# Weight halves of the FFN steps moved between the gate's operations on VectorE and ScalarE

## The reference

```python
def adaln_in(x, g, m, i):                       # first block
    return rmsnorm(x, g) * (1 + m[:, i, 1][:, None]) + m[:, i, 0][:, None]

def swiglu(h, w1, w3, w2):
    return (jax.nn.silu(h @ w1) * (h @ w3)) @ w2

m = (cond @ w_mod[l] + b_mod[l]).reshape(bsz, 3, 3, D_MODEL)
x = x + 0.5 * m[:, 0, 2][:, None] * swiglu(adaln_in(...), ffn_w1, ffn_w3, ffn_w2)   # first block
h = h + 0.5 * swiglu_2(rmsnorm_2(h, g[0]), ffn_w1, ffn_w3, ffn_w2)                  # second block
```

## Time and profile before

| | |
|---|---|
| median of 3 runs | 1780.08 us |
| the profiled execution | 1783.61 us, span 1781.8 us |
| TensorE (PE) busy | 1501.1 us, 84% |
| VectorE (DVE) busy | 1397.3 us, 78% |
| ScalarE (ACT) busy | 986.8 us, 55% |
| DMA | 420.30 MB, 236 GB/s in the mean |
| low halves (L1957) on VectorE | 418 of the pairs and 205 of block 2, about 1220 ns each |
| high halves (L1444) on ScalarE | 418 and 209, about 1046 ns each |

### The profile page before, as it was taken

How to read it: one execution, slowest core, us unless ns; L and a number is a source line. 1 busy time by engine, 2 the same in 40 slices (tenths; PEclk the granted TensorE clock), 3 DMA queues, 4 the chain that set the end, 5 groups by cost and what they waited for, 6 DMA issues and landing times.

```text
span 1781.8 us, 27728 instructions
## 1 busy us (share of the span) xinstructions
PE 1501.1 (84%) x11160; PEld 1416.2 (79%) x11160; DVE 1397.3 (78%) x2275; ACT 986.8 (55%) x1643; POOL 9.8 (1%) x24
## 2 busy tenths in 40 slices
PE   5988778788878888886998997997998899788997
PEld 4988667677868786866998997887998799767996
DVE  7598866789988998867888777786777777786776
ACT  4444535554555445536666556555555655675554
POOL 0000000000000000000000000000000000000000
PEclk8699878898988998998999998998999899899999
DMA  8599863579967994425896775336677577425763
GB/s 332 207 365 376 313 207 124 204 262 337 325 239 283 377 375 157 162 99 211 303 334 218 246 248 198 143 113 231 233 243 245 190 249 247 157 82 211 242 244 107
DMA packets 84972, 420.30 MB, mean 236 GB/s; under 512 B 9363, under 2 KB 9795, under 8 KB 58094
## 3 DMA queue, kind: packets, MB, share of 16 engines
q1 hardware_dynamic: 82910, 410.59, 63.6%
q0 software_dynamic: 1936, 7.95, 1.3%
HBM read 417.37 MB, written 1.13 MB: 235 GB/s over the span
## 4 chain that ended last, share of the span: by engine, by line
DVE 55%; ACT 16%; PE 16%; issue 6%; DMA 6%; SPq 0%; DVEq 0%
DVE low_p L1957 19%; DVE low_d L1957 11%; DVE modw L1790 7%; ACT hi_p L1444 6%; ACT a_hi L1467 4%; PE pw L624 4%; DVE gu L2085 3%; PE pw L625 3%; DVE gu L2077 3%; PE acc L624 3%; PE acc L625 3%; DMA land_p<-stream 2%; ACT gu L1462 2%; DMA land_d<-stream 2%; DMA biasT<-wmod 2%
## 5 line engine op out<-in xcount | busy, mean ns | idle before, releaser
L624 PE MATMUL pw<-h_hi,hi_p 128*128 128x256 f32 x2928 | 760.3, 297 | 129.7 <-DVE low_p L1957 113.2
L625 PE MATMUL pw<-h_lo,low_p 128*128 128x256 f32 x2928 | 739.8, 290 | 0.0
L624 PEld LDWEIGHTS pw<-h_hi,hi_p 128*128 128x128 f32 x2928 | 584.6, 200 | 166.2 <-DVE low_p L1957 116.2
L625 PEld LDWEIGHTS pw<-h_lo,low_p 128*128 128x128 f32 x2928 | 585.0, 200 | 0.4 <-issue 0.2
L1957 DVE SCALAR_TENSOR_TENSOR low_p<-hi_p,land_p 128x1024 fp32r<-128x1024 f32 x418 | 494.0, 1220 | 107.5 <-ACT hi_p L1444 107.4
L1444 ACT ACTIVATE hi_p<-land_p 128x1024 fp32r<-128x1024 f32 x418 | 418.1, 1045 | 90.0 <-DMA land_p<-stream 89.9
L624 PE MATMUL acc<-a_hi,hi_d 128*128 128x256 f32 x1376 | 357.0, 294 | 54.4 <-DVE low_d L1957 54.4
L625 PE MATMUL acc<-a_lo,low_d 128*128 128x256 f32 x1376 | 354.0, 292 | 0.0
L624 PEld LDWEIGHTS acc<-a_hi,hi_d 128*128 128x128 f32 x1376 | 278.1, 202 | 57.4 <-issue 57.4
L625 PEld LDWEIGHTS acc<-a_lo,low_d 128*128 128x128 f32 x1376 | 278.2, 202 | 0.0
L1957 DVE SCALAR_TENSOR_TENSOR low_d<-hi_d,land_d 128x1024 fp32r<-128x1024 f32 x205 | 249.5, 1218 | 9.2 <-ACT hi_d L1444 9.1
(11 more groups left out here) (354 smaller groups left out, 1723.6 us busy)
## 6 DMA issues: line engine op xcount, KB each, us to landing
land_p<-stream SPq DMA_DIRECT2D x207, 1024.0 KB, 5.1
land_d<-stream SPq DMA_DIRECT2D x209, 512.0 KB, 5.7
modw<-wmod SPq DMA_DIRECT2D x124, 512.0 KB, 5.7
biasT<-wmod SPq DMA_DIRECT2D x20, 512.0 KB, 7.4
biasT<-bias_rows POOLq DMA_DIRECT2D x3, 1536.0 KB, 11.7
biasT<-bias_rows POOLq DMA_DIRECT2D x1, 3072.0 KB, 12.9
land_p<-stream SPq DMA_DIRECT2D x4, 512.0 KB, 7.3
cst_s<-cst SPq DMA_DIRECT2D x1, 1792.0 KB, 10.0
```

The lines of the kernel that those rows point to most:

```text
L624: mm(o, lhs[0], rhs[0], start=start, stop=False, skip_group_check=True)
L625: return mm(o, lhs[1], rhs[1], start=False, stop=stop, skip_group_check=True)
```

## The change

In every FFN step but the first few of a stage (`smooth`), the halves of the weights are placed elsewhere in the same order of blocks. On ScalarE the first high half of the step goes between silu and `a_hi`. On VectorE the first low half goes between the gate and `a_lo`, the second low half of the pair behind `a_lo`, the modulation blocks behind that, and the low half of block 2 goes into the next step, between its scale and its gate (in the first block's stages, where there is no scale, at the head of the next step). In the last step of a stage block 2 is split at the end. What is computed stays the same, as do the loads and TensorE's order.

```diff
@@ -97,6 +97,13 @@
 
 
 ENTRY, STEPS, OWN, LEAVE = split_groups()
+
+
+def smooth(i, j):
+
+    return j >= (UNSHIFTED if i == 0 else 2 if i in RAW else 1 if i >= 6 else 0)
+
+
 BEGIN = [(0, 0), (0, 1), (1, 0), (1, 1), (2, 0), (2, 1), (0, 2)]
 SPLITS = list(BEGIN)
 for _i, (_kind, _blocks) in enumerate(STAGES):
@@ -1463,12 +1470,14 @@
                 else:
                     act.wait_ge(gu_ready, f * NFF + j + 1)
                     fn(sig[0:r, j % 2, :], pw[j % (LAG + 1)][0:r, 0:S], ACT.Silu).then_inc(silu_done, 1)
+                between = STEPS[i, j][0:1] if smooth(i, j) else []
+                split_high(between)
                 act.wait_ge(gated_ready, f * NFF + j + 1)
                 fn(a_hi[0:r, j % (LAG + 1), :], act_in[0:r, j % 2, :], ACT.Copy, scale=ONCE).then_inc(a_hi_ready, 1)
                 if i == j == 0:
                     hidden_plain(range(KD))
                 if j or not deferred(i):
-                    split_high(STEPS[i, j])
+                    split_high(STEPS[i, j][len(between):])
 
             split_high(BEGIN[0:2])
             squares(0)
@@ -2076,6 +2085,8 @@
                         dve.wait_ge(gu_ready, f0 + j + 1)
                         v.tensor_tensor(gu[:, j % 2], pw[j % (LAG + 1)][:].rearrange("p (b s) -> p b s", b=2),
                                         rs[:].unsqueeze(1).to_broadcast([P, 2, S]), ALU.mult).then_inc(scaled, 1)
+                    if smooth(i, j) and smooth(i, j - 1):
+                        split_low(STEPS[i, j - 1][-1:])
                     dve.wait_ge(silu_done, f0 + j + 1)
                     if t0 + j > LAG:
 
@@ -2083,6 +2094,8 @@
                     r = unit_rows(t0 + j)
                     up_half = act_in[:, j % 2, :] if deferred(i) else pw[j % (LAG + 1)][:, S:2 * S] if r == P else pw[j % (LAG + 1)][r:P, 0:S]
                     v.tensor_tensor(act_in[0:r, j % 2, :], sig[0:r, j % 2, :], up_half, ALU.mult).then_inc(gated_ready, 1)
+                    if smooth(i, j):
+                        split_low(STEPS[i, j][0:1])
                     dve.wait_ge(a_hi_ready, f0 + j + 1)
                     low_act = a_lo[:, j % (LAG + 1), :] if r == P else a_hi[r:P, j % (LAG + 1), :]
                     v.scalar_tensor_tensor(low_act, act_in[0:r, j % 2, :], TWICE, a_hi[0:r, j % (LAG + 1), :], ALU.mult, ALU.subtract).then_inc(act_ready, 1)
@@ -2092,10 +2105,14 @@
                         filter_sums()
                     if i == 2 and j == TAP_AT[-1] + 3:
                         filter_squares()
+                    if smooth(i, j):
+                        split_low(STEPS[i, j][1:-1])
+                    elif j or not deferred(i):
+                        split_low(STEPS[i, j])
                     if j < NFF - 1:
                         mods(i, j)
-                    if j or not deferred(i):
-                        split_low(STEPS[i, j])
+                    else:
+                        split_low(STEPS[i, j][-1:])
 
                 gated(0)
 
```

## The result

The change makes the kernel faster: 1737.36 us in the median of 4 runs (1735.33 to 1741.39) against 1779.98 before, a ratio of 0.9766 with a 95% interval of 0.9746 to 0.9787. The prediction was 1706. The gain is 43 us where 74 were forecast. The median itself stands just inside the end of the range at 1738; taken as a ratio, 0.9766 of the 1780.08 given is 1738.4, just past it.

What follows compares the result with a forecast made beforehand. VectorE was taken to set the pace in the late stages, DMA to limit stages 0 and 3. Savings of 69 + 1 + 4 = 74 us from the profiled 1783.6 gave 1709.6, or 1706 against the median; range 1683 to 1738.

Steps and rivals of the forecast that it cites:

- Late stages: Stages 6, 8, 9, 11: step falls from VectorE's 6.44 us to TensorE's 5.76, starts and ends shorten; 69 us saved.
- Stage 5: TensorE is full there, so only the last low half comes earlier: 1 us saved, between 0 and 2.
- (c): Waits only change place, ScalarE gives the high half late, VectorE stays near 6.4 us: -5, 1775 us; chance 0.04.
- (d): Late stages: TensorE's clock falls under unbroken work, at 0.85 a step is 6.78 us: slower, 1802 us; chance 0.03.
- Stages 0, 2 and 3: Early stages: covered waits stand against DMA; change of 0 in stages 0 and 3, -4 us in stage 2.
- the prediction's own mark of being wrong: The forecast is wrong if, among other signs, stages 0 and 3 move by more than 8 us either way.
- rival (b): Early stages: queue loop holds, loads go out late, steps take 7.85 us: 1759, or 1733 at half price; chance 0.20.
- a step longer than 6.75 empties it: Early stages: longer steps empty the full DMA queue, so pair loads land in 7.05 us, not 8.7.
- between DMA's own 6.75 and 7.0: Early steps with two modulation blocks: predicted length in us, around today's 6.94.
- the prediction's own formula: Early stages' pair-load loop over two steps: 0.95 to issue, landing, 1.1 high half, 4.95 to the blocks' end; halved per step.
- DMA as the bound: Early stages: at 388 GB/s and share 1.00, a step with two modulation blocks cannot go under 6.75 us.
- (a): DMA is no limit; stages 0, 2, 3 gain all their waits, 23 us more, 1683 us; chance 0.13.

Runs made afterwards that it cites:

- down_ahead: The change with the modulation loads' due time 0.6 later, so the down load stands ahead of them on SP, the pair load still behind; 1706.81 us.
- small_mods_after: The change with modulation loads of groups 3 to 5 and 9 to 16 cut to an eighth of their columns, the product scaled by 0.05; 1697.62 us.
- mods_first: The change with the modulation blocks directly behind the gate, ahead of the first low half; 1677.48 us, 0.942 of the kernel before.
- the repaired kernels: The change with modulation blocks right behind the gate (1677.48 us), or with modulation loads one step later in SP's order (1675.93 us).

## Why the prediction was wrong

**Late stages: right, to 1 us.** Forecast 69, measured 70.0. The step is 5.76; the stages gain 18.1, 18.0, 18.6 and 15.2 us for 18.2 three times and 14.8. The terms hold as well as their sum: in stage 6 the start came 0.88 earlier for 0.9, and the end 5.0 for 5.1. VectorE's own pace was 4.73 for 4.85. Stage 5 gave 1.3 for 1. Rivals (c) and (d) are out: no wait took the place of the old ones in these stages, and the granted clock stayed at 1.00 there at 98 us of work in 98, against 1.00 at 112.9 in 123. The Trainium skill (TensorE: Matmul & The Clock Gate, Part 1) has activity release the throttle; stage 6 of the change agrees.

**Stages 0, 2 and 3: the step that failed.** The sum took 0, -4 and 0 for them; they came out at +11.6, +6.2 and +7.7, which is nearly all of the 31 us between the forecast gain and the measured one. Stage 0 also passed the prediction's own mark of being wrong, 8 us. The mechanism was on the page, as rival (b): the modulation blocks end later in the step, SP holds the pair load behind them, and the high half that needs it is wanted sooner. Its price was 49 us at full size and the measured loss is half of that. It counted 18 steps with two blocks at +0.91 in each of the three stages; there are 18, 15 and 11 of them, and they became 0.71, 0.52 and 0.73 us longer in the mean, while the steps with three blocks in stage 3, 8.08 us before, hardly changed (all but the last).

What failed is the sentence "a step longer than 6.75 empties it", with the landing of 7.05 us that follows, and so the step "between DMA's own 6.75 and 7.0". The pair loads of the change land in 8.2 us in the median in stage 3, and in 8.7 in stage 0 from 100 to 128 us, the 8.7 of the earlier trace rows unchanged. At 8.2 the prediction's own formula gives (0.95 + 8.2 + 1.1 + 4.95)/2 = 7.6, and the steps with two blocks are 7.68 in the mean in stage 3. In stage 0, 16 of the 18 are 7.65 in the mean, where the formula gives 7.85 at 8.7; two of over 10 us, as long before, are left out.

One turn of it in the trace: the blocks end at 104.56, SP issues the pair load at 105.52, it lands 8.2 us later at 113.7, ScalarE makes its first high half at 113.77 and VectorE the low half at 114.93, behind the gate, and the blocks of that step end at 119.88. That is 15.3 us for two steps, 7.66 each. The four pair loads of the earlier trace rows's window differ, though: 8.2, 6.6, 9.4 and 9.1 us in the change.

The down load closes a second loop of its own that the prediction did not count: 0.48 to its issue, some 6.6 to land, 1.1 for the high half, and 6.4 of VectorE's work to the end of the blocks, 14.6 or an estimated 7.3 a step. down_ahead showed that freeing it gives 25.4 of the 58 us, not far from half.

VectorE's, ScalarE's and SP's rows of that turn in the change:

```profile
104.56 0.08 DVE L1799 DVE_READ_ACCUMULATOR modw<-modw,condb 128x1 f32 x1
...
105.32 1.23 DVE L1966 SCALAR_TENSOR_TENSOR low_d<-hi_d,land_d 128x1024 fp32r<-128x1024 f32 x1 [0.48 <-ACT hi_d L1451]
...
108.56 1.23 DVE L1966 SCALAR_TENSOR_TENSOR low_p<-hi_p,land_p 128x1024 fp32r<-128x1024 f32 x1 [1.68 <-ACT hi_p L1451]
...
114.60 0.41 DVE L2096 TENSOR_TENSOR gu<-gu,pw 128x256 f32<-128x256 f32 x1
114.93 1.22 DVE L1966 SCALAR_TENSOR_TENSOR low_p<-hi_p,land_p 128x1024 fp32r<-128x1024 f32 x1
...
119.88 0.08 DVE L1799 DVE_READ_ACCUMULATOR modw<-modw,condb 128x1 f32 x1
```

```profile
113.77 1.06 ACT L1451 ACTIVATE hi_p<-land_p 128x1024 fp32r<-128x1024 f32 x1 [1.12 <-DMA land_p<-stream]
```

```profile
103.53 1.47 SPq L518 DMA_DIRECT2D modw<-wmod  x2
105.04 0.43 SPq L538 DMA_DIRECT2D land_d<-stream  x1
105.52 0.43 SPq L531 DMA_DIRECT2D land_p<-stream  x1
```

**Why the landing did not fall.** The four loads of a step are still issued within 2 us of each other, and the pair is the last of them; its landing is then that of the whole batch. Cutting the batch (small_mods_after) brought it to 5.8. The working took 6.75 us for the batch and fixed costs from a lone pair, and came out 1.2 to 1.7 us short. That it is the batch is what the cut loads suggest; what the missing 1.2 to 1.7 us are was not found, and the loads were not tried one by one.

**DMA as the bound: wrong.** The prediction took the share of 1.00 at 388 GB/s for a ceiling and 6.75 us as the least a step with two blocks could take. mods_first runs such steps in 6.37 at 412 GB/s. That error hid the other: with the ceiling believed, the gain of (a) looked out of reach and the loop looked harmless. The Trainium skill, which was weighed there (DMA: Bandwidth & Descriptors, "Where 436 GB/s comes from"), gives 435 GB/s as the ceiling of the fabric. The 412 of mods_first do not reach that figure, and no run here shows it. The prediction also had the trace disagree with the 358 GB/s of the Trainium skill (the same page); but that figure is for two cores that both stream, and only one runs here, so no run tests it. The prediction had set beside it that VectorE's 6.46 would then decide, and mods_first bears that out with 6.37; but not for the order as it was changed.

**The forecast for rival (a)**, 23 us more, was the right reading of VectorE's waits: the repaired kernels save 33 us in the three stages against before, 10 to 12 each, where it counted 9.

## What to carry to other kernels

Before moving work later on an engine, list what its completion releases on the issuing queue, and everything queued behind that: here two passes that ended 1.7 us later in the step delayed loads of quite another tensor, and the repair needed no engine to change, only the order of the issues. A loop through such a queue is best priced with the landing time as measured in that stretch: here it stayed at 8.2 to 8.7 us though the step grew and the share fell. A DMA share of 1.00 was no ceiling in this kernel; what showed it was a run that asked for more.

## What was not expected of the hardware

The DMA share reads 1.00 at 388 GB/s, 1.02 at 412 and 0.98 at 372, so near 1 it tells little on what is left. And two covers of the same chain of hops (waits for ScalarE and back) are worth more together (1.71 us) than their sum (0.58 and 0.57): moving the down half in front of the gate also gives ScalarE the time for the high half that the next cover needs.
